# A gather that ends in two halves around the first expert product, and expert places counted from one

## The reference: what is computed

```
h = x + mixer(rms_norm(x))                 # convolution, linear recurrence, pooling, gates
u = rms_norm(h)
group  = argmax over 4 group logits of u   # softmax weight of the group
top 2 of that group's 8 experts            # softmax over the two
h = h + sum over the token's 2 experts of weight * expert(u)
    expert(u) = (silu(u @ w_gate[e]) * (u @ w_up[e])) @ w_down[e]
h = h + sigmoid(rms_norm(h) @ w_ple_gate) * (p @ w_ple);  out = rms_norm(h)
```

## Time and profile before

| what | value |
|---|---|
| three timed executions | 881.57, 883.30, 883.87 us (median 883.3) |
| the profiled execution | 881.89 us, of which its instructions span 880.1 us |
| TensorE busy, weight loads busy | 834.1 us (95%), 523.1 us (59%) |
| VectorE, ScalarE, GpSimd busy | 340.0, 270.5, 91.4 us |
| moved by the DMA engines | 253.33 MB, mean 288 GB/s |
| mean granted TensorE clock | 0.988 of full speed |

### The profile page before, as it was taken

The page is one execution under the profiler, slowest core; times in us unless marked ns, Lnnn a source line. Parts: engine busy times, 40 slices in busy tenths (PEclk is TensorE's granted clock), DMA queues, the critical chain, the costliest instruction groups (busy, mean ns, idle before and its releaser), DMA issues.

```text
span 880.1 us, 10387 instructions
## 1 busy us (share of the span) xinstructions
PE 834.1 (95%) x4297; PEld 523.1 (59%) x4297; DVE 340.0 (39%) x484; ACT 270.5 (31%) x393; POOL 91.4 (10%) x68
## 2 busy tenths in 40 slices
PE   7999999999999999999999999989899797789996
PEld 5888888788888888536535354353353353333686
DVE  7899449962652615411020120101101202005765
ACT  7666347733332236202020200101001001000777
POOL 3436370000000003000000000000000000001000
PEclk9999999999999999999999999999899999999998
DMA  8222222211525766799999999999999999999902
GB/s 241 102 85 96 96 95 96 96 49 49 190 96 203 293 269 265 289 426 425 398 425 432 426 427 428 425 428 430 428 428 426 428 426 429 428 421 363 355 5 95
DMA packets 45192, 253.33 MB, mean 288 GB/s; under 512 B 8853, under 2 KB 9945, under 8 KB 31834
## 3 DMA queue, kind: packets, MB, share of 16 engines
q1 hardware_dynamic: 42696, 248.21, 69.5%
q0 software_dynamic: 2304, 4.20, 1.2%
q10 hardware_dynamic: 146, 0.27, 0.1%
HBM read 246.37 MB, written 10.49 MB: 292 GB/s over the span
## 4 chain that ended last, share of the span: by engine, by line
PE 70%; DMA 17%; SPq 5%; DVE 4%; ACT 3%; issue 2%; DVEq 0%; ACTq 0%
PE bank L1507 68%; DMA ring<-in_w_down_e_dram 14%; DMA ring<-in_w_ple_gate_dram 2%; SPq L519 1%; SPq L630 1%; DVE ring L1178 1%; DVE ring L1158 1%; PE bank L1761 1%; SPq L532 1%; DMA ring<-in_w_in_dram 1%; ACT ring_rounded L414 0%; PE bank L1864 0%; SPq L527 0%; PE bank L1580 0%; ACT ring L799 0%
## 5 line engine op out<-in xcount | busy, mean ns | idle before, releaser
L1507 PE MATMUL bank<-ring_rounded,ring_rounded 128*128 128x512 f32 (+1 forms) x696 | 244.4, 389 | 0.2 <-DVE ring_rounded L1169 0.2
L1507 PE MATMUL bank<-r_rounded,ring_rounded 128*128 128x512 f32 (+1 forms) x744 | 234.4, 389 | 0.4 <-DVE ring_rounded L1113 0.4
L1507 PEld LDWEIGHTS bank<-r_rounded,ring_rounded 128*128 128x128 f32 x744 | 138.9, 188 | 30.2 <-DVE ring_rounded L1113 0.6
L1507 PEld LDWEIGHTS bank<-ring_rounded,ring_rounded 128*128 128x128 f32 x696 | 130.5, 188 | 27.8 <-issue 0.7
L1507 PE MATMUL bank<-ring,gain 128*64 128x512 f32 x472 | 119.7, 612 | 17.4 <-issue 16.1
L1507 PE MATMUL bank<-ring,hT 128*64 128x512 f32 x400 | 111.0, 617 | 6.3 <-DMA ring<-in_w_down_e_dram 6.3
L1507 PE MATMUL bank<-ring,junk 128*64 128x512 f32 x472 | 115.5, 592 | 0.0
L1507 PEld LDWEIGHTS bank<-ring,gain 128*64 128x64 f32 x472 | 36.8, 140 | 84.2 <-issue 81.7
L974 ACT ACTIVATE r<-bank,factor 128x512 f32<-128x512 f32 x16 | 11.0, 687 | 233.0 <-PE bank L1507 233.0
L1507 PEld LDWEIGHTS bank<-ring,junk 128*64 128x64 f32 x472 | 37.9, 137 | 70.9 <-issue 70.8
L1386 DVE TENSOR_SCALAR r<-bank,factor 128x512 f32<-128x512 f32 x16 | 12.0, 751 | 154.6 <-PE bank L1507 154.6
(11 more groups left out here) (239 smaller groups left out, 775.1 us busy)
## 6 DMA issues: line engine op xcount, KB each, us to landing
ring<-in_w_up_e_dram SPq DMA_DIRECT2D x29, 2048.0 KB, 29.6
ring<-in_w_gate_e_dram SPq DMA_DIRECT2D x24, 2048.0 KB, 27.8
ring<-in_w_down_e_dram SPq DMA_DIRECT2D x22, 2048.0 KB, 31.4
ring<-in_w_in_dram SPq DMA_DIRECT2D x18, 1024.0 KB, 7.3
r<-in_w_gate_e_dram SPq DMA_DIRECT2D x5, 2048.0 KB, 25.7
r<-in_w_down_e_dram SPq DMA_DIRECT2D x4, 2048.0 KB, 33.6
ring<-in_w_down_e_dram SPq DMA_DIRECT2D x7, 1024.0 KB, 29.8
ring<-in_w_up_e_dram SPq DMA_DIRECT2D x6, 1024.0 KB, 10.8
```

What stands on the lines that cost most here:

```text
L1507: return nc.tensor.matmul(*a, **k)
```

## The change

Three edits are made.

1. `iota` starts at 1. `find_places` writes (count + 1) times the mark straight into `place`, and the instruction that took one away is gone. An unused expert now has place 0. `rcount`, the table 1/1 to 1/16 of the pooling, is the reciprocal of `iota` itself, so that the instruction that added one is gone too. The arg-max helper also reads `iota`, as a ranking alone.
2. `rows_split` takes a range of k-tiles, and tile 3's call becomes two calls of four k-tiles each, each with its own increment of `rows_low_ready`.
3. The first team's gather: after tile 2 of all k-tiles, a function `gather_last_tile(half)` does tile 3 of four k-tiles, the rounded parts, then the remainders. Its first half stands ahead of the first gate product, its second half inside it, after its fourth k-tile.

```diff
-        def rows_split(eng, api, i):
+        def rows_split(eng, api, i, ks=slice(0, KD)):
...
-            api.tensor_tensor(rows_low(i), h1_by_k(i), rows_high(i), ALU.subtract).then_inc(rows_low_ready, 1)
+            api.tensor_tensor(rows_low(i)[:, ks, :], h1_by_k(i)[:, ks, :], rows_high(i)[:, ks, :],
+                              ALU.subtract).then_inc(rows_low_ready, 1)
...
-            nc.gpsimd.iota(iota[:, :], pattern=[[1, C]], base=0, channel_multiplier=0,
+            nc.gpsimd.iota(iota[:, :], pattern=[[1, C]], base=1, channel_multiplier=0,
...
-            after(v.tensor_scalar(rcount[:, :], iota[:, 0:PAD], 1.0, None, ALU.add))
-            v.reciprocal(rcount[:, :], rcount[:, :]).then_inc(prm_ready, 1)
+            v.reciprocal(rcount[:, :], iota[:, 0:PAD]).then_inc(prm_ready, 1)
...
-                after(v.scalar_tensor_tensor(out=cand[:, at, :],
+                after(v.scalar_tensor_tensor(out=place[:, 0:NE, at].rearrange("p e i -> p i e"),
...
-                after(v.tensor_scalar(place[:, 0:NE, at].rearrange("p e i -> p i e"), cand[:, at, :], -1.0, None, ALU.add))
...
-            rows_split(dve, v, TT - 1)
+            rows_split(dve, v, TT - 1, slice(0, KD // 2))
+            rows_split(dve, v, TT - 1, slice(KD // 2, KD))
...
                 for k in range(KD):
                     gather_k(bank[4 + k // 2], k, TT - 2, start=False, stop=False)
-                    gather_k(bank[4 + k // 2], k, TT - 1, (rows_high,), start=False, stop=False)
-                pe.wait_ge(rows_low_ready, TT)
-                for k in range(KD):
-                    ins = gather_k(bank[4 + k // 2], k, TT - 1, (rows_low,), start=False, stop=(k % 2 == 1))
-                    if k % 2 == 1:
-                        ins.then_inc(xT_psum, 1)
+
+                def gather_last_tile(half):
+                    ks = range(half * KD // 2, (half + 1) * KD // 2)
+                    for k in ks:
+                        gather_k(bank[4 + k // 2], k, TT - 1, (rows_high,), start=False, stop=False)
+                    pe.wait_ge(rows_low_ready, TT + half)
+                    for k in ks:
+                        ins = gather_k(bank[4 + k // 2], k, TT - 1, (rows_low,), start=False, stop=(k % 2 == 1))
+                        if k % 2 == 1:
+                            ins.then_inc(xT_psum, 1)
+
+                gather_last_tile(0)
                 pe.wait_ge(rounds_ready, 1)
-                gate_or_up(r, n0, 0, 0)
+                gate_or_up(r, n0, 0, 0, midway=lambda: gather_last_tile(1))
```

## The result

The changed kernel takes 883.58 us (median of 13 executions, 882.76 to 885.65), the kernel before on the same chips 882.46 (13 executions, 881.39 to 883.87). The ratio is 1.0015 with a 95% interval of 1.0008 to 1.0022: 1.3 us slower, 0.7 to 1.9. That is small, but clear of no difference. The profiled execution took 883.92 us, its instructions span 882.2.

What follows compares the result with a forecast made beforehand. The expert stage was taken as bound by its matrices' transfer. Gate start 0.91 us earlier and end 0.60 later were to move the end by 0.0 us (-0.8 to +0.7): 883.3 us, range 881.0 to 885.3.

Steps and rivals of the forecast that it cites:

- Places, table and split remainder: Ahead of the gate: second half's places gain 0.26 us; table gains nothing; split remainder covered by 0.7 us and more.
- The two waits for ScalarE: TensorE waits for ScalarE's copy: 0.33 us ahead of the gate's start, 0.24 us ahead of its second half.
- The earlier start: First gate product starts 0.91 us earlier, the stream too, which spends that 0.9 us dry waiting for the gate's end.
- the gate's end: End of the first gate product, and all behind it on TensorE, 0.60 us later.
- The upper bound of 1.35 us: Gate's end 1.35 us late instead of 0.60 if each change of tiling mode cost its upper bound, 0.52.
- The stream goes on then, just where it stood before: At the third issue, 367.85, data flow about 369.5, when the first two issues were through before: end moves 0.0 us.
- Behind it the backlog grows, as 523.17 shows.: After the two whole matrices issued at 382.74 the transfer queue stays filled; a transfer of 31.41 us at 523.17 shows it.
- the middle between 0.9 and 2.4 us: Delay from SP's issue to data, taken midway between two bounds: data first moving, 0.9, and 336 GB/s reached, 2.4.
- The break in the gate passes through: Rival: stream runs dry at the third issue and at 382.74, end comes with TensorE: +0.7, 884.0 us; chance 0.17.
- All of the early start stays: Rival: third batch finds the queue just short of empty, stream stays 0.9 us early throughout: 882.4 us; chance 0.18.
- The gap of 2.91 us at 571.98: Rival: a TensorE gap without a shown releaser moves, shifting the end by 3 us: 880.4 or 886.2; chance 0.10.
- the gate did start earlier: Against the rival that `rounds_i` or ScalarE's first copy comes late, the stream losing 0.6: 883.9 us; chance 0.05.

Runs made afterwards that it cites:

- the half releases: First halves of two matrices issued once pair 1's down product has done two of four k-tiles; on the kernel before alone: -0.5 us (-1.3 to +0.3).
- the late first loads: Kernel before, SP's first two issues waiting for the gate's k-tile 3 instead of 1: first issue 1.72 us late, stream 0.07 us behind at 40 MiB.

## Why the prediction was wrong

The forecast was no change at 883.3 us. The time itself, 883.58, is inside the range, but the kernel became slower by 1.3 us (0.7 to 1.9) where no change was forecast. That the time lies so near is luck in part: the median of the kernel before turned out 0.8 lower than the 883.3 that it was counted from.

**What held.** Places, table and split remainder cost and gain what was said: the gather starts 1.05 us behind the places' start instead of 1.27, 0.22 against 0.26 forecast (0.05 less because the write with gaps takes 0.27 us, not 0.22). The first half gained nothing: its comparison now starts at once and takes 1.57 us instead of 0.69, until GpSimd is done. The two waits for ScalarE, the changes of tiling and the order of the terms were there as described. The earlier start was indeed lost.

**The mis-sized term: the gate's end, +0.60 forecast, +0.91 measured.** The forecast took 0.39 us for one of ScalarE's copies, a quarter of the 1.57 that four take. But the copies overlap, and each takes longer than its quarter (ns min/median/max, first and last start):

```profile
L961 ACT ACTIVATE gain<-bank,gain_col x4: 466/476/485, 359.3 to 360.4; 128x256 f32<-128x256 f32 x4
```

That is 0.09 us more, twice; from the copy's end the product follows after 0.05, much as forecast. In the middle, besides, the second product of the gather starts 0.22 us behind its first (363.38 and 363.61), not 0.12. So the start came 0.09 later than worked out and the middle took 1.55 instead of 1.41; 0.04 each came from the places and the second half's own length. The upper bound of 1.35 us was also worked out wrongly: the second change of tiling would have filled the wait for ScalarE, not come on top of it, so by the prediction's own terms it is 1.11.

**The step that failed** is what the stream makes of it: "The stream goes on then, just where it stood before", and for 382.74 "Behind it the backlog grows, as 523.17 shows." Neither is so. At the two places named the stream loses more than the middle between 0.9 and 2.4 us says: with issues 0.91 later it is 0.55 late at 8 MiB and 1.26 at 9. The third issue's first packet does start 0.95 us behind it (368.62 and 369.57), near the lower bound; but the rate rises slowly. From the 0.55 an estimate of the delay is 1.9 us instead of the 1.65 of the middle: counted from the places the issue comes at 13.33, and before the change the first two issues are through at 369.5, which is 14.67; 13.33 + 1.9 is 0.55 behind that. Even so these places don't set the end. The backlog doesn't grow from 385 to 523: it is nearly used up at 434, where the rate falls to 287 GB/s, and from there the stream goes by TensorE's time in every kernel without the half releases. Up to that point TensorE waits for no load (from the first gate product's end to 520 the view of waits shows no matmul that waits, before and after), so its 0.91 arrives whole.

The sign of it stood in the earlier trace rows: the 20th slice, 418 to 440 us, has 398 GB/s, the weakest of the nineteen between 374 and 792 us, and the prediction took it into "between 398 and 432". An average of 7% less over 22 us is a stop of 1.5 us, which is what the half releases gave back to the stream.

**The rivals.** "The break in the gate passes through" had the outcome and nearly the price (+0.7 forecast, +0.9 in the stream), and by the estimate of 1.9 us its point of decision, 1.65 upward, was passed. But the cost reaches the end in another way: not the time from issue to data decides, but a place where the queue is nearly empty in any case. "All of the early start stays" is refuted: the stream was 0.9 us late, and with the late first loads it ended where it does without them. The gap of 2.91 us at 571.98 stands in the changed trace too (3.29 us at 573.34), and the gate did start earlier. On the rule of the Trainium skill (TensorEngine Tiling (Array Packing), Key Properties, a change of mode empties the engine) the traces agree with the small price: 0.12 and 0.18 us.

## What to carry to other kernels

Where a stage is bound by transfers, look for the *last* place where their queue runs nearly empty, by the windows' rate in steps of a few us over the whole stage: all that happens ahead of it counts only through the engine that ends the emptiness. An earlier first issue is worth nothing as long as such a place lies behind it, and a later product in the engine's list is carried through in full. Splitting work to start something earlier also adds a latency for each piece (here twice 0.4 us of waiting for ScalarE's copy); fill that wait with work which is due anyway, or don't split.

## What the runs showed of the hardware

A comparison on VectorE with both inputs in the core's memory is held up by GpSimd's subtraction. The changed kernel's first half, VectorE and then GpSimd:

```profile
347.30 0.27 DVE L1279 SCALAR_TENSOR_TENSOR place<-bank,sig 128x64 f32<-128x64 f32 x1
347.60 1.57 DVE L1288 TENSOR_TENSOR pick<-iota,place 128x512 fp32r<-128x512 f32 x1
```

```profile
345.75 2.87 POOL L441 TENSOR_TENSOR r_rounded<-r,r_rounded 128x1024 fp32r<-128x1024 f32 x1 [5.68 <-issue]
```

The instruction with one input from the accumulator's bank runs in 0.27 us beside GpSimd; the comparison, 0.69 us elsewhere, ends at 349.17, 0.55 us behind GpSimd's end at 348.62. The Trainium skill (SBUF — State Buffer, Who interferes with whom) says that a VectorE instruction with two such inputs contends with a GpSimd instruction that reads the same memory. The trace agrees, with 0.9 us of delay.

ScalarE's copies of 128x256 overlap: each takes 0.47 to 0.48 us, and yet four end 1.57 us behind the first one's start, because the next starts 0.36 to 0.37 us behind the one ahead. So a quarter of such a row is the step and not the length. The handover from a copy to a waiting product took 0.05 us (359.27 + 0.48 = 359.75, 359.80), as did that from VectorE's comparison (355.60 + 0.69 = 356.29, 356.34).

Transfers come up slowly behind a dry place. In the kernel before the packets of 16 KiB took 0.61 us ahead of 435, and those under way at 435.75 took 1.09. The windows view hides this: in it a packet's time is booked to one window, so that the half microsecond from 435.50 has a busy share of 1.88, and the 0.94 beside 303 GB/s from 434 to 436 doesn't mean that the engines were busy throughout.
